# Value weights of the compression: the first half is loaded into free rows of the softmax tile, the second into the columns that the key weights' first half leaves

## The reference

```python
def compress_blocks(x, pe, w1, w2):
    ...
    blocks = blocks + pe[None, None, :, None, :].astype(x.dtype)
    flat = jnp.moveaxis(blocks, 3, 2).reshape(B, n_cmp, H, CMP_BLOCK * D)
    return jax.nn.silu(flat @ w1) @ w2

k_cmp = compress_blocks(kv[:, :, 0], cmp_pe[0], cmp_w1[0], cmp_w2[0])
v_cmp = compress_blocks(kv[:, :, 1], cmp_pe[1], cmp_w1[1], cmp_w2[1])
```

## Time and profile before

| | us |
|---|---|
| median of 3 runs | 1393.94 |
| lowest and highest run | 1391.26 and 1396.41 |
| span of the profiled execution | 1392.0 |
| TensorE busy in it | 1271.4 |
| DVE, ACT and POOL busy | 779.1, 340.8 and 246.0 |

### The profile page before, as it was taken

The page is one execution under the profiler, slowest core; times in us unless marked ns, Lnnn a source line. Parts: engine busy times, 40 slices in busy tenths (PEclk is TensorE's granted clock), DMA queues, the critical chain, the costliest instruction groups (busy, mean ns, idle before and its releaser), DMA issues.

```text
span 1392.0 us, 26288 instructions
## 1 busy us (share of the span) xinstructions
PE 1271.4 (91%) x10100; PEld 1023.5 (74%) x10100; DVE 779.1 (56%) x1634; ACT 340.8 (24%) x895; POOL 246.0 (18%) x316
## 2 busy tenths in 40 slices
PE   7996898967997999999999999978785899999998
PEld 4453676645896888899999955656452568999998
DVE  1805646574666661576875448559342307677753
ACT  2114534432332221100000011359532311000000
POOL 1103000044342420111210111240112111112100
PEclk9998899988998999999999999979997999999999
DMA  8437797887355762354535433350247653444451
GB/s 291 143 109 267 243 335 266 272 272 242 122 159 180 258 217 98 122 181 131 172 104 189 163 122 121 118 137 1 78 141 241 200 170 124 147 157 157 131 167 35
DMA packets 151839, 236.11 MB, mean 170 GB/s; under 512 B 10627, under 2 KB 114307, under 8 KB 151299
## 3 DMA queue, kind: packets, MB, share of 16 engines
q1 hardware_dynamic: 140066, 204.14, 44.4%
q0 software_dynamic: 7488, 28.21, 6.0%
q10 hardware_dynamic: 4160, 2.10, 0.6%
HBM read 229.09 MB, written 13.64 MB: 174 GB/s over the span
## 4 chain that ended last, share of the span: by engine, by line
PE 81%; DVE 5%; ACT 4%; SPq 3%; DMA 3%; issue 3%; POOL 0%; POOLq 0%; ACTq 0%; DVEq 0%
PE ps L799 20%; PE ps L582 11%; PE ps L827 11%; PE ps L547 10%; PE ps L893 9%; PE ps L765 5%; PE ps L777 2%; PE ps L689 2%; PE ps L741 2%; ACT big L1160 2%; SPq L406 2%; PE ps L588 1%; PE ps L1024 1%; DMA proj<-in_cmp_w 1%; PE ps L905 1%
## 5 line engine op out<-in xcount | busy, mean ns | idle before, releaser
L893 PE MATMUL ps<-big,proj 128*128 128x168 f32 (+1 forms) x1024 | 160.1, 309 | 10.0 <-DMA proj<-in_cmp_w 8.2
L547 PE MATMUL ps<-ct,ring 128*128 128x128 f32 x960 | 147.0, 293 | 22.4 <-DMA ring<-in_cache_kv 9.6
L547 PEld LDWEIGHTS ps<-ct,ring 128*128 128x128 f32 x960 | 113.4, 148 | 66.8 <-issue 42.7
L582 PE MATMUL ps<-ring,xT 128*128 128x512 f32 (+1 forms) x384 | 158.9, 570 | 0.9 <-DMA ring<-in_w_in 0.9
L893 PEld LDWEIGHTS ps<-big,proj 128*128 128x128 f32 x1024 | 149.3, 192 | 13.3 <-DMA proj<-in_cmp_w 8.4
L582 PEld LDWEIGHTS ps<-ring,xT 128*128 128x128 f32 x384 | 69.4, 191 | 78.0 <-issue 76.3
L799 PE MATMUL ps<-kT,proj 128*128 128x144 f32 x960 | 124.1, 286 | 0.0
L799 PEld LDWEIGHTS ps<-kT,proj 128*128 128x128 f32 x960 | 120.3, 190 | 0.0
L1160 ACT ACTIVATE big<-ps 128x512 f32<-128x512 f32 (+3 forms) x172 | 87.5, 532 | 126.8 <-PE ps L547 125.9
L2109 POOL TENSOR_TENSOR big<-rows 128x576 f32<-128x576 f32 x22 | 51.0, 2317 | 261.4 <-DVE rows L1739 228.1
L799 PE MATMUL ps<-xT,ring 128*128 128x144 f32 x640 | 84.9, 286 | 0.0
(11 more groups left out here) (298 smaller groups left out, 2094.3 us busy)
## 6 DMA issues: line engine op xcount, KB each, us to landing
ring<-in_cache_kv SPq DMA_DIRECT2D x128, 512.0 KB, 5.7
ring<-in_w_gu SPq DMA_DIRECT2D x44, 1024.0 KB, 7.7
ring<-in_w_in SPq DMA_DIRECT2D x11, 2048.0 KB, 8.1
ring<-in_w_down SPq DMA_DIRECT2D x16, 1408.0 KB, 6.6
ring<-in_cache_kv SPq DMA_DIRECT2D x120, 128.0 KB, 3.4
ring<-in_cache_kv POOLq DMA_DIRECT2D x120, 128.0 KB, 3.1
ring<-in_w_out SPq DMA_DIRECT2D x4, 2048.0 KB, 11.3
out<-in_state_win POOLq DMA_DIRECT2D x8, 1016.0 KB, 19.5
```

The costliest lines, as they stand in the source:

```text
L547: return nc.tensor.transpose(out, in_, C("ident", 0, rows, rows))
L582: last = mm(ps[b + t][:, 0:w], xT[:, k, t * P:(t + 1) * P], src[:, k, :], start=k == 0, stop=k == KD - 1)
L893: last = mm(cmp_out(u, si, n), w1s(s, o)[:, hf * P:(hf + 1) * P], XS[(4 * kp + si) % XB][:, o, 0:n], start=o == 0, stop=o == 7)
```

## The change

`w1v` replaces `w1s` for products of passes 4 to 7. The first half of the value weights (columns 0 to 127) no longer goes into columns of `proj` but into the softmax tile: the upper eight blocks to row 1 and the lower eight to row 0, columns 0 to 1023. The second half (columns 128 to 255) goes into columns 0 to 127 of each block in `proj`, where the first half of the key weights stood until product 27. `sum_w1` reads the raw blocks at their new places, and writes sums and differences where it did before.

The transfers are the same four of 512 KB on ACT's queue. The first now stands ahead of `double(4)` (product 19, with a wait for `r_w[0]`), the second ahead of `double(5)` (product 23, with a wait for `r_t[0]`), and the two of the second half ahead of `double(6)` (product 27, with the wait `c_h` 28).

```diff
+        def w1v(s, o, hf):
+            if s in (1, 2):
+                return w1s(s, o)[:, hf * P:(hf + 1) * P]
+            if hf == 1:
+                return w1s(s, o)[:, 0:P]
+            return R[:, 1 if s == 0 else 0, o * P:(o + 1) * P]
...
-                    last = mm(cmp_out(u, si, n), w1s(s, o)[:, hf * P:(hf + 1) * P], XS[(4 * kp + si) % XB][:, o, 0:n],
+                    w = w1s(s, o)[:, hf * P:(hf + 1) * P] if kp < 4 else w1v(s, o, hf)
+                    last = mm(cmp_out(u, si, n), w, XS[(4 * kp + si) % XB][:, o, 0:n],
...
-            def load_value_weights(hf):
-                cols = slice(hf * P, (hf + 1) * P)
-                act.wait_ge(c_h, 28 + 4 * hf)
+            def load_value_block(t):
+                if t == 0:
+                    act.wait_ge(r_w[0], 3)
+                else:
+                    act.wait_ge(r_t[0], 9)
+                act.dma_start(R[:, 1 - t, 0:8 * P].rearrange("p (i n) -> p i n", n=P),
+                              w1_h[:, 1, 8 * t:8 * t + 8, 0:P]).then_inc(s_w1, 16)
+            def load_second_half():
+                act.wait_ge(c_h, 28)
                 for t in range(2):
-                    act.dma_start(proj[:, t, 0:8 * CH].rearrange("p (i n) -> p i n", n=CH)[:, :, cols],
-                                  w1_h[:, 1, 8 * t:8 * t + 8, cols]).then_inc((s_w1, s_w2)[hf], 16)
+                    act.dma_start(proj[:, t, 0:8 * CH].rearrange("p (i n) -> p i n", n=CH)[:, :, 0:P],
+                                  w1_h[:, 1, 8 * t:8 * t + 8, P:2 * P]).then_inc(s_w2, 16)
...
-                        if u in (6, 7):
-                            load_value_weights(u - 6)
+                        if u in (4, 5):
+                            load_value_block(u - 4)
+                        if u == 6:
+                            load_second_half()
                         double(u)
...
                 cols = slice(hf * P, (hf + 1) * P) if k else slice(0, CH)
+                raw = slice(0, P) if k else cols
                 def part(t, c):
+                    if k and not hf and c < 8:
+                        return R[:, 1 - t, c * P:(c + 4) * P].rearrange("p (i n) -> p i n", n=P)
+                    return proj[:, t, c * CH:(c + 4) * CH].rearrange("p (i n) -> p i n", n=CH)[:, :, raw]
+                def total(t, c):
                     return proj[:, t, c * CH:(c + 4) * CH].rearrange("p (i n) -> p i n", n=CH)[:, :, cols]
...
-                tt(part(2, 0), part(0, 0), part(1, 0), ALU.add)
...
+                tt(total(2, 0), part(0, 0), part(1, 0), ALU.add)
```

More of the change, by code:

```diff
@@ L1855, in sum_w1 @@
                     dve.wait_ge(c_h, 28 + 4 * hf)
-                tt(part(2, 0), part(0, 0), part(1, 0), ALU.add)
-                tt(part(2, 4), part(0, 4), part(1, 4), ALU.add).then_inc(c_b, 1)
-                tt(part(0, 8), part(0, 0), part(1, 0), ALU.subtract)
-                tt(part(1, 8), part(0, 4), part(1, 4), ALU.subtract).then_inc(c_b, 1)
+                tt(total(2, 0), part(0, 0), part(1, 0), ALU.add)
+                tt(total(2, 4), part(0, 4), part(1, 4), ALU.add).then_inc(c_b, 1)
+                tt(total(0, 8), part(0, 0), part(1, 0), ALU.subtract)
+                tt(total(1, 8), part(0, 4), part(1, 4), ALU.subtract).then_inc(c_b, 1)
             def combine(u):
```

## The result

The changed kernel takes 1383.4 us (median of 4 runs, 1380.4 to 1385.0) against 1394.58 for the kernel before (4 runs): a ratio of 0.993, with a 95% interval of 0.9901 to 0.996. Run again with the experiments, beside 20 runs of the kernel before on the same chip, it has a ratio of 0.9909 (0.9886 to 0.9933). The forecast was 1384, in a range of 1380.5 to 1389.

The account below looks back on a forecast made before the run. TensorE, 91% busy, and its holes were taken to bound the kernel. Removing wait and clock loss (-10.9 us) and giving back 0.9 made -10.0, from 1393.9 to 1384 us, range 1380.5 to 1389.

Parts of the forecast that it names:

- The hole and the clock: TensorE's wait for weights before product 32 (8.18 us) and the lowered clock behind it (2.71) both go: -10.9 us.
- B: Stretch from product 32 to the line 741 attention step behind product 34; 9.10 us at full clock without any wait.
- Given back to DVE: After product 32, TensorE's next turn waits for a page copy that DVE makes only after its weight sums: +0.9 us.
- Early issues on ACT: Issuing two transfers near products 19 and 23 takes ACT about 0.5 us each and costs TensorE nothing: 0.
- Early transfers on the DMA engines: From 384 to 412 us the engines have 15 us of room for 3.8 us of early weight transfers: cost 0.
- second half: Asked for at product 27, it lands about 430.0, ahead of DVE's sum at 431.7 and product 36 at 438.7: cost 0.
- Later loads move along: Behind products 34 and 36, cache pieces land in time and later loads move earlier with TensorE's freed slots: no cost.

Follow-up runs that it names:

- All at 27: Changed kernel with all four weight transfers asked for at product 27, first half still into the softmax tile: 1392.5 us, ratio 0.9991 to the kernel before.
- second half only: Against the changed kernel, halves swapped: second into the softmax tile at products 19 and 23, first into its old columns at 27: 1390.2 us, ratio 0.9965.
- one block early: Changed kernel with only the first half's upper block asked for at product 19, its lower block back at 27: 1382.1 us, ratio 0.9934 to the kernel before.
- Split sums: Changed kernel with DVE's first-half weight sums split, additions after product 31, subtractions after 33: 1383.5 us, ratio 0.993 to the kernel before.
- Block twice: Changed kernel with the first half's upper block read at product 19 and again at 23: 1381.5 us, ratio 0.9929 to the kernel before.
- second late: Changed kernel with the second half asked for at product 35 instead of 27: 1395.8 us, ratio 1.0027 to the kernel before.
- again: The changed kernel rerun unchanged as a base on the experiments' chip: 1384.1 us, ratio 0.9909 to the kernel before.

## Why the prediction was right

**The hole and the clock (-10.9).** Right. Product 32 comes 8.35 us earlier against product 28 where the prediction had 8.18, and the clock's share, from B of the kernel before and B without waits, is 2.55 where it had 2.71; together 10.9 again. "All at 27", "second half only" and "one block early" show the cause from three sides.

**Given back to DVE (+0.9).** Right in place, kind and size: 0.90 for the copy of line 1845, predicted as 424.63 to 425.53 and measured, less the 3.3 us of later start, at 424.6 to 425.5. "Split sums" removed it, and gave back 10.28 - 9.19 = 1.1 us. Measured B is 10.28 against the 10.0 worked out; the step of line 749 came at 435.29 - 3.28 = 432.0 where 431.9 was forecast. That so short a wait leaves the clock alone was assumed, since no row of the prediction has a wait of that length; it came out so.

**Early issues on ACT (0).** Right. Each took 0.4 us. The first slipped in between two copies, at 383.1 on the clock of the old profile and so 0.8 us sooner than forecast, and the `double` behind it still had 0.38 us of idling, as in the earlier trace rows.

**Early transfers on the DMA engines (0), second half (0).** Right. The second half, asked for at 416.05, landed at 432.9, or 429.6 on the clock of the old profile, against 430.0. "Block twice" put half a MB more beside the cache loads, and no wait of TensorE up to product 32 came of it.

**Later loads move along (0).** The one step with a hole in it. The cache piece of pass 6 was late in the changed kernel's profile:

```profile
457.48 0.66 PE L555 MATMUL ps<-ct,ring 128*128 128x128 f32 x4 [0.95 <-DMA ring<-in_cache_kv]
```

SP asks for twelve transfers in a row there, most of them 1.1 us apart, and their last issue stands at the same distance behind the step of line 741 in all traces (19.0 to 19.1 us), while TensorE wants the piece 21.1 us behind that step where nothing delays it ("second half only"). The landing decides by tenths: it came 21.2 us behind the step in the profile of the kernel before, 22.2 in that of the changed one, and 21.0 to 22.0 in the others (leaving out "second late"). The loads do move along, and the race between them and TensorE was there already. What it costs differs from trace to trace, and the traces are too few to say that the change makes it dearer: from product 32 into pass 6 TensorE waits 0 to 1.5 us for cache pieces over all eleven, 1.0 in "second half only", which has the old hole.

In sum the stage is 8.35 + 1.46 - 0.93 = 8.9 us shorter in the two first profiles, against 10.0 forecast. In "again" it is 9.2, or 8.2 with the wait in pass 6 behind it. The medians fell by 11.2 and 9.8. That the first of them met the forecast of 1384 within 0.6 us, with 1.1 us less from the stage than forecast, is luck: the interval of its ratio leaves 6 to 14 us. Single profiles differ by several us in stretches that the change doesn't touch. The stage begins 3.3 us later in the changed kernel's profile, and layer 1 is 3.4 us shorter: 5.0 us at the last scores of the prompt's attention, 1.1 at 1003 us of the old profile, 3.4 at the end. Stretches from 900 to 960 us of the kernel before and of the changed one:

```profile
900.00:960.00 60.00, 46.74 (x366) 34.50 (x365) 38.81 (x128) 42.34 (x164) 21.86 (x50) 0.86 0.37 106
```

```profile
900.00:960.00 60.00, 44.39 (x405) 33.74 (x404) 48.97 (x161) 46.89 (x196) 16.69 (x40) 0.94 0.28 77
```

The clock there is granted at 0.86 in one and 0.94 in the other (the same instructions stand 6 to 11 us earlier in the second). Over all eleven traces the stretch from layer 1's first matmul to the last scores of its prompt attention takes 164.6 to 169.6 us, with the same instructions; the kernel before has the longest. The profile of "second half only" ends 3.8 us earlier than that kernel's, and 3.7 of it come in layer 1. That its median came out low may be this, but one profile of each doesn't settle it.

## What to carry to other kernels

When the columns that a load needs are free too late, look for a tile of another stage that is dead at that time: the transfer was free once it was asked for 38 and 30 us ahead, and the gain was the wait plus a quarter to a third of it in clock. Count the queued work behind a stall before you remove it: the engine that idled in the same hole (here DVE, with 2.5 us of sums) becomes late next. Spread the issues of one queue; a third one in a row held ACT for 2.6 us. And compare single profiles by the starts of the same instructions in the stage that was changed: their whole spans differ by several us for other reasons.

## What the runs showed of the hardware

An issue on ACT took 0.4 us with no earlier transfer of 512 KB under way on its queue, 0.6 to 1.6 us with one, 2.6 to 2.7 us as the third of a row and 4.4 us in the kernel before with two under way, and 9.9 us as the fourth of a row. The landing of the same transfer took 4.0 to 4.3 us at product 19, where the engines had been idle, and 16.8 to 17.2 us as the second of a row at product 27, beside 4.2 MB of cache loads; the first of that row took 5.4 to 7.9.

A wait of 2.03 us of TensorE was followed by the lower clock level ("one block early", 0.54 of full speed); waits of 0.9 to 1.0 us for the same copy in five traces were not. The clock's loss was 1.7 us behind the wait of 2.0, 2.55 behind 8.2, 2.7 behind 7.8 ("second half only") and 3.0 behind 12.1: it grew far less than the wait.
